# One step list for gates, heads and page products in a decoder kernel, with squares added in pairs and page numbers read in four parts

## The chip, the cores and the metric

The kernel runs on one core of one Trainium2 chip. The time is device microseconds of one execution; 1627.98 us is the median of three runs of the kernel before (1627.06 to 1630.11). One further execution was taken with the hardware profiler, and all rows below are from it.

## What is computed

Two layers of a decoder trunk, run in one step on 256 tokens of one prompt and 4 new tokens of each of 8 samples (288 columns in all), D = 1024. Everything is float32.

```python
x += 0.5 * SwiGLU_1(rmsnorm(x))                         # FF = 2816
h = rmsnorm(x) @ w_in                                   # a_u, a_v, q, k, v, c_q, and three gates of 1024
u, v_n = gelu(a_u), layer_norm(gelu(a_v))
y_a = u * chunk_spatial_gate(v_n, s_w, s_b)             # 4 groups of 128, chunks of 128
y_b = moba_attention(rope(q), rope(k), v, past pages)   # 8 heads of 64; samples: 1024 past keys in pages of 128
y_c = cross_attention(c_q, memory keys, memory values)  # 4 heads of 128, 256 memory rows
g_a, g_b, g_c = split(sigmoid(gates), 3)
merged = g_a * (y_a @ w_a) + g_b * (y_b @ w_b) + g_c * (y_c @ w_c)
x += merged @ w_o
x += 0.5 * SwiGLU_2(rmsnorm(x))
```

After two layers a last rmsnorm gives y; new keys, values, memory keys and values and the samples' v_n are outputs too. `page_table` says which physical page of the cache each logical page of a sample is.

## The kernel before

All activations lie feature-major: 128 partitions, chunks of 288 columns. A weight matrix is walked in **units**: half a tile of 256 output columns by up to 1024 rows, 448 units for two layers (`layer_units`, 224 a layer). SP loads each unit into one of NR = 6 buffers (`load`), waiting until the unit six before it is used. ACT copies it rounded to the high half (`hi`, into one of NH = 4 buffers, L810), DVE subtracts for the low half (`lo`, L1110), and TensorE (`half`, L413) runs three matmuls of 288 columns per 128x128 block: high by high, low activation by high, high by low. A whole half tile is 24 matmuls; a half of w_a_out, w_b_out or w_c_out is 12. Results go to two pairs of PSUM banks, `res` slot 0 and slot 1; `evac[s]` counts how often slot s was taken, and the first matmul of a tile waits for it. Four more banks `gb` serve everything else in an order that `bank_uses` lists.

Each engine's order is its program's order: five programs, held together by semaphores alone. A layer is: feed-forward 1 (units 0 to 67), memory keys and values (68 to 75), the twelve tiles of w_in that are not gates (76 to 99, with the key pages of the samples between them), `attention_a` (100 to 115), `attention_c` (116 to 139), w_b_out (140 to 147), w_o (148 to 155), feed-forward 2 (156 to 223).

**The mean of squares.** ACT squares two chunks of x at a time into `work` (L830, `square`), 1/D included. When all four pairs are there DVE sums the eight chunks into `sqs` with one tensor_reduce (L1137, `sum_squares`), at the head of the next stage; TensorE sums over partitions with one float32 matmul against ones (L447, `sum_of`) placed behind the first tile of that stage. The same form serves layer norm (L1345, L1364) and the memory (L1168).

**attention_a** has 14 steps. In step n TensorE computes the scores of head n (L669), then one third of a gate step (two half tiles of a gate of branch a in slot 0, then the w_a_out tile in slot 1, for g = 0 to 3), then transposes the probabilities of head n-1 (L476), a quad of memory pages, and the output of head n-2 (L689, L697). Steps 12 and 13 finish heads 10 and 11 and have no gate work. DVE per step: scale the scores and find their maximum (L1424 or L1426, L1428), invert the sum and normalise the head before (L1440, L1442), the low half of a weight unit or the gate times branch product (L1451), copy a head's output out (L1460). ACT per step: weights' high half or sigmoid of the gate (L821), exp (L1010), copy of the transposed probabilities (L1021). Sigmoid, exp and sqrt each want their table loaded first.

The branch input goes through `high` (ACT, L984) and `y_low` (DVE, L1394), and w_a_out's first tile waits for `y_lo`. **attention_c** does the same for the memory branch (12 thirds of gate steps), with one quad of value pages beside each, then the four gate tiles of branch b, then waits for `y_lo` of the attention branch. DVE `select(1)` chooses the blocks of the second group of samples between the two.

**w_b_out, w_o.** Each w_b_out tile goes DVE product, DVE sum into `merged` (L1548, L1551), ACT high half (L1070), DVE low half (`merged_low`, L1538), between `hi` and `lo` of coming units. The first half tile of w_o needs the first two groups of merged (`m_lo` 2), the second all four.

**Pages.** A quad is four pages of 256 KB for four samples; `HOMES` gives the buffer of each. SP loads 24 quads a layer between weight units (`quad`, at unit numbers written out in `A_AT` and `C_AT`), POOL 16. Page numbers are read into SP's registers once, all eight quads' worth of two groups in a row, behind the load of unit 12 of layer 0 (L1590).

Of the kernel before, what the change touches and what calls it, by code (L numbers as in the profile page):

```python
# [6 lines left out]
F32 = mybir.dt.float32  # L7
# [6 lines left out]
P = 128  # L14
# [74 lines left out]
FFN_UNITS, LAYER_UNITS = 68, 224  # L89
U_MEM, U_QK, U_SLOT, U_GA, U_GC, U_SIGB, U_BRB, U_WO, U_FFN2 = 68, 76, 84, 100, 116, 132, 140, 148, 156  # L90
DOWN_NK = [8, 8, 6]
SLOT_TILES = [8, 9, 2, 3, 0, 1, 10, 11]


def layer_units():
# [12 lines left out]
    def gate(j, g):  # L108
        return tile("w_in", g + (GATE0 + j * D) // W)
# [8 lines left out]
    for j, name in ((0, "w_a_out"), (2, "w_c_out")):  # L118
        for g in range(4):
            u += gate(j, g) + tile(name, g, 0, 4)  # L120
    for g in range(4):
        u += gate(1, g)
    for g in range(4):
        u += tile("w_b_out", g, 0, 4)
    for t in range(4):
        u += tile("w_o", t)
# [24 lines left out]
HOME_NAMES = ("X", "Y", "Q0", "Q1", "Q2", "Q3", "W")  # L151

# [20 lines left out]
def bank_uses():  # L173

    def layer(L):
# [6 lines left out]
        for n in range(HEADS + 2):  # L182
# [5 lines left out]
            u += [("mo1", 3)] if n == 10 else []  # L188
            u += [(f"O{n - 2}", 2)] if n >= 2 and (n >= 10 or n % 2 == 0) else []
        u += [("moT", 0), ("oG0", 2), ("pTa1", 0), ("pTb1", 1), ("pTn1", 3), ("oT0", 0), ("oG1", 2), ("oT1", 0), ("rs2", 1)]  # L190
# [30 lines left out]
def build(nc, A):  # L221
# [158 lines left out]
    def _(pe):  # L380
# [62 lines left out]
        def sum_of(name, n, count):  # L443

            claim(name)
            pe.wait_ge(*count)
            pe.matmul(bk(name)[:, 0:n], ones, sqs[:, 0:n], start=True, stop=True).then_inc(filled_of(name), 1)  # L447

        def ffn(L, f):
            F = 2 * L + f - 1  # L450
            for i in range(UP):
                tile(0, 8, normed, ready=(lambda k: pe.wait_ge(norm_ready, 8 * F + k + 1)) if i == 0 else None)
                if i == 0:
                    if F == 0:
                        pe.wait_ge(ld_const, 16)
                    sum_of(f"rs{f}.{L}", T, (sqs_ready, 3 * L + (1 if f == 1 else 3)))
                if i == 2 and F == 0:
                    claim("memsum.0")
                    pe.wait_ge(memsum_ready, 1)
                    pe.matmul(bk("memsum.0")[:, 0:MEM], ones, mrstd[:], start=True, stop=True)\  # L460
                        .then_inc(filled_of("memsum.0"), 1)
# [56 lines left out]
        def mix(L):  # L518
# [17 lines left out]
            sum_of(f"rsm.{L}", T, (sqs_ready, 3 * L + 2))  # L536
# [61 lines left out]
            sum_of(f"ln1.{L}", T, (ln_sum, 2 * L + 1))  # L598
# [6 lines left out]
            sum_of(f"ln2.{L}", T, (ln_sum, 2 * L + 2))  # L605
# [28 lines left out]
            attention_a(L, spatial)  # L634
            attention_c(L)
# [13 lines left out]
        def gate_step(L, m, j, nth):  # L649

            if m % 3 < 2:
# [1134 lines left out]
```

## Time and profile before

| | |
|---|---|
| median of 3 runs | 1627.98 us (1627.06 to 1630.11) |
| the profiled execution | 1631.34 us, span of its trace 1629.7 us |
| TensorE busy | 1554.3 us (95%) |
| DVE, ACT, POOL busy | 916.8, 697.2, 80.9 us |
| mean granted TensorE clock | 0.976 of full |
| chain that ended last, by engine | TensorE 89%, DVE 6%, ACT 2% |

The page gives busy time, a row of 40 slices, the chain of work that ended last, and the costliest groups of instructions with the idle time just before them and who ended it. Views of the trace give the same for a stretch, an engine or a tile, and the instructions one by one. Start times are microseconds from the start of the span. A matmul's busy time includes its way through the array, so the pace of matmuls is read from their starts.

### The profile page before, as it was taken

The page shows a single profiled execution, that of the slowest core. Times are in us where ns is not written, and L with a number is a line of the kernel's source. Part 1 is how long each engine was busy: PE and PEld are TensorE (multiplying, and loading weights), DVE is VectorE, ACT ScalarE, POOL GpSimd, SP SyncE. Part 2 cuts the span into 40 slices and gives each one's busy share as a digit, 9 for nine tenths or more (in the row PEclk, how much of TensorE's full clock was granted, in tenths as well). Part 3 has the DMA queues.
Part 4 walks back from the last instruction along what each step waited for, and adds up shares of the span by engine and source line. Part 5 has one row for each costly group of instructions (what it writes and reads, how often), then busy time and mean ns, then how long its engine had stood idle before and what let it go on. Part 6 is the DMA issues. An engine that isn't in the chain of part 4 may idle for free.

```text
span 1629.7 us, 28853 instructions
## 1 busy us (share of the span) xinstructions
PE 1554.3 (95%) x12164; PEld 1470.2 (90%) x12164; DVE 916.8 (56%) x1169; ACT 697.2 (43%) x907; POOL 80.9 (5%) x153
## 2 busy tenths in 40 slices
PE   7799999999999989999999999999999997999996
PEld 7799999997877889999999999999977777999996
DVE  6566447564644366665466654665656435755644
ACT  6344335354543344444344443433555333544432
POOL 0000000130003000000000000004000210000000
PEclk9899999999999999999999999999999998999998
DMA  6345658695479344445544456759655853444552
GB/s 246 117 165 160 208 178 288 237 329 167 155 251 337 107 159 153 165 168 155 168 166 161 166 188 191 240 196 350 232 181 175 324 207 130 155 161 164 161 166 78
DMA packets 106001, 313.86 MB, mean 193 GB/s; under 512 B 12880, under 2 KB 12880, under 8 KB 105744
## 3 DMA queue, kind: packets, MB, share of 16 engines
q1 hardware_dynamic: 94320, 273.87, 50.5%
q0 software_dynamic: 11552, 38.15, 6.3%
q8 instruction: 96, 1.57, 0.4%
q14 instruction: 33, 0.27, 0.1%
HBM read 306.20 MB, written 5.77 MB: 191 GB/s over the span
## 4 chain that ended last, share of the span: by engine, by line
PE 89%; DVE 6%; ACT 2%; issue 1%; SPq 1%; DMA 1%; DVEq 0%; ACTq 0%
PE res L413 76%; PE gb L497 2%; PE gb L506 2%; DVE square_sums L1137 2%; PE gb L669 2%; PE res L435 1%; PE gb L476 1%; ACT whi L810 1%; DVE wlo L1110 1%; DMA wraw<-in_ffn_w 1%; SPq L1590 1%; PE gb L697 1%; PE gb L689 1%; PE gb L489 1%; PE gb L447 1%
## 5 line engine op out<-in xcount | busy, mean ns | idle before, releaser
L1110 DVE TENSOR_TENSOR wlo<-wraw,whi 128x1024 fp32r<-128x1024 f32 (+2 forms) x448 | 512.0, 1148 | 552.9 <-ACT whi L810 551.9
L413 PE MATMUL res<-norm_hi,whi 128*128 128x288 f32 x2176 | 659.8, 303 | 21.0 <-DVE wlo L1110 10.0
L810 ACT ACTIVATE whi<-wraw 128x1024 fp32r<-128x1024 f32 (+2 forms) x448 | 443.5, 994 | 540.2 <-PE res L413 497.8
L413 PE MATMUL res<-norm_lo,whi 128*128 128x288 f32 x2176 | 646.3, 297 | 0.0
L413 PE MATMUL res<-norm_hi,wlo 128*128 128x288 f32 x2176 | 644.1, 296 | 0.0
L413 PEld LDWEIGHTS res<-norm_hi,whi 128*128 128x128 f32 x2176 | 412.6, 190 | 48.4 <-issue 24.0
L413 PEld LDWEIGHTS res<-norm_lo,whi 128*128 128x128 f32 x2176 | 413.3, 190 | 1.1
L413 PEld LDWEIGHTS res<-norm_hi,wlo 128*128 128x128 f32 x2176 | 413.9, 190 | 0.0
L413 PE MATMUL res<-h_hi,whi 128*128 128x288 f32 x1024 | 311.3, 304 | 22.3 <-DVE h_lo L1394 13.1
L413 PE MATMUL res<-h_lo,whi 128*128 128x288 f32 x1024 | 307.9, 301 | 0.0
L413 PE MATMUL res<-h_hi,wlo 128*128 128x288 f32 x1024 | 307.2, 300 | 0.0
L413 PEld LDWEIGHTS res<-h_hi,whi 128*128 128x128 f32 x1024 | 197.7, 193 | 31.9 <-DVE h_lo L1394 14.3
L413 PEld LDWEIGHTS res<-h_hi,wlo 128*128 128x128 f32 x1024 | 198.3, 194 | 0.0
L413 PEld LDWEIGHTS res<-h_lo,whi 128*128 128x128 f32 x1024 | 198.0, 193 | 0.1
L871 ACT ACTIVATE h_hi<-hf 128x576 fp32r<-128x576 f32 x44 | 30.2, 687 | 96.6 <-DVE hf L1188 96.6
L856 ACT ACTIVATE sil<-scaled 128x576 f32<-128x576 f32 x44 | 30.2, 685 | 86.5 <-DVE scaled L1165 86.5
L1010 ACT ACTIVATE soft<-soft,stat 128x256 f32<-128x256 f32 x48 | 24.1, 502 | 39.5 <-DVE stat L1428 39.4
L1679 POOL MEMSET q_blockdiag<- 128x512 f32 x8 | 3.9, 523 | 624.9 <-DVE h_lo L1150 619.1
L830 ACT ACTIVATE work<-x_T 128x576 f32<-128x576 f32 x28 | 18.7, 676 | 35.2 <-DVE x_T L1132 35.2
L1150 DVE TENSOR_TENSOR h_lo<-hf,h_hi 128x576 fp32r<-128x576 f32 x44 | 33.1, 752 | 0.0
L1165 DVE TENSOR_TENSOR scaled<-res,rstd 128x576 f32<-128x576 f32 x44 | 33.0, 750 | 0.1
L1132 DVE SCALAR_TENSOR_TENSOR x_T<-res,x_T 128x288 f32<-128x288 f32 x48 | 19.7, 452 | 23.7 <-PE res L413 23.5
(189 smaller groups left out, 1125.1 us busy)
## 6 DMA issues: line engine op xcount, KB each, us to landing
wraw<-in_ffn_w SPq DMA_DIRECT2D x240, 512.0 KB, 3.5
wraw<-in_w_in SPq DMA_DIRECT2D x96, 512.0 KB, 5.0
wraw<-in_ffn_w SPq DMA_DIRECT2D x32, 384.0 KB, 3.2
page_Q<-in_cache_k POOLq DMA_DIRECT2D x48, 256.0 KB, 5.1
page_Q<-in_cache_k SPq DMA_DIRECT2D x40, 256.0 KB, 5.0
page_Q<-in_cache_v SPq DMA_DIRECT2D x40, 256.0 KB, 5.4
wraw<-in_w_mem_kv SPq DMA_DIRECT2D x16, 512.0 KB, 3.4
page_Q<-in_cache_v POOLq DMA_DIRECT2D x32, 256.0 KB, 5.1
```

The costliest lines, as they stand in the source:

```text
L413: mm = pe.matmul(res[:, 2 * s + c, 0:n], w_, m_, start=begin and k == 0 and j == 0, stop=end and k == kh - 1 and j == 2)
L497: mm = pe.matmul(bk(name)[32 * e:32 * e + 32, col:col + P], q_[:, c, e, :], page[b][e][:, c * P:(c + 1) * P], start=c == 0, stop=c == 3)
L506: mm = pe.matmul(bk(name)[32 * e:32 * e + 32, :], probs[:, 32 * e:32 * e + 32], page[b][e][:], start=begin, stop=end)
L669: mm = pe.matmul(bk(nm)[:, qt * 256:(qt + 1) * 256], lhs, rhs, start=True, stop=True)
L810: act.activation(whi[n % NH][:, 0:kh, :], wraw[n % NR][:, 0:kh, :], ACT.Copy).then_inc(hi_done, 1)
L856: act.activation(sil[:], scaled[:], ACT.Silu).then_inc(sil_ready, 1)
L871: act.activation(hh[:, 2 * i:2 * i + 2, :], hf[:], ACT.Copy).then_inc(hh_ready, 1)
L1010: a = act.activation(soft[n % 2][:, qt, :], soft[n % 2][:, qt, :], ACT.Exp, bias=stat[:, 4 * (n % 2) + qt:4 * (n % 2) + qt + 1], accum_out ...
L1110: dve.tensor_tensor(wlo[n % NR][:, 0:kh, :], wraw[n % NR][:, 0:kh, :], whi[n % NH][:, 0:kh, :].bitcast(F32), ALU.subtract).then_inc(lo_don ...
L1137: dve.tensor_reduce(sqs[:], work[:, 0:chunks, :].rearrange("p k t -> p t k"), AX.X, ALU.add).then_inc(sqs_ready, 1)
L1150: dve.tensor_tensor(hl[:, 2 * i:2 * i + 2, :], hf[:], hh[:, 2 * i:2 * i + 2, :].bitcast(F32), ALU.subtract)\
L1165: dve.tensor_tensor(scaled[:], rs(0), both(rstd[:]), ALU.mult).then_inc(evac[0], 1)
```

## The change

**One step list.** `attention_a` and `attention_c` become one loop `gates` over 32 steps (`STEPS`): capital letters are half gate tiles, small letters whole branch tiles. Per branch two gates (four halves) come first, and each product stands behind a later gate. Heads are steps 0 to 11, their tails fall in steps 12 and 13 beside the gates of the memory branch; value quads are steps 12 to 19 and 21 to 28; the last memory product (c, 3) moves behind the gates of b. The weight units are laid out in this order. Branch b's input takes the place of branch a's in h. SP's places for quads come from the last use of each buffer (`load_after`). DVE takes a head's output one step later, `spatial` behind the normalising of a head, `y_low` for branch a in step 3, ACT's `high` for it in step 2.

**Squares in pairs.** `sum_squares` goes. DVE adds pairs of chunks into the first pair as they come (`add_squares`): group 1 behind the third tile of the projection, group 2 behind the fourth, group 3 at the head of the next stage. TensorE sums over partitions with two matmuls. Layer norm's two sums and the memory's go the same way. At the end the third group's sum is done as before by TensorE, and a Sqrt on one column is put ahead of the last `deviation`.

**Page numbers in four parts**, behind the loads of units 12, 16, 20 and 24 of layer 0; the loads of sgu_b and sgu_w move to unit 28.

**Also**: w_o's halves run (0,0) (1,0) (0,1) (1,1) and then as before, and the new x is taken at the halves where a tile ends; at the start each weight unit's halves follow one pair of chunks of x, not two; memory's high and low halves are made two per pass in passes 6 to 9 of feed-forward 1, not one in passes 3 to 10, and the memory is scaled in pass 3, not 2.

```diff
+def gate_steps(b):
+    two = [(b, g, h) for g in range(2) for h in range(2)]
+    return two + [(b.lower(), 0, None), (b, 2, 0), (b, 2, 1), (b.lower(), 1, None), (b, 3, 0), (b, 3, 1), (b.lower(), 2, None),
+                  (b.lower(), 3, None)]
+
+
+STEPS = gate_steps("A") + gate_steps("C")[:-1] + [("B", g, h) for g in range(4) for h in range(2)] + [("c", 3, None)]
+N_STEPS = len(STEPS)
+WO_ORDER = [(0, 0), (1, 0), (0, 1), (1, 1), (2, 0), (2, 1), (3, 0), (3, 1)]
...
+QUAD_STEP = {Q_MK + i: 1 + i for i in range(4)}
+QUAD_STEP.update({Q_MV + i: 8 + i for i in range(4)})
+QUAD_STEP.update({Q_V + i: 12 + i + i // 8 for i in range(16)})
+
+
+def quad_unit(q):
+    return U_SLOT + q if q < Q_MK else step_unit(QUAD_STEP[q] + 1) - 1
+
+
+FIRST_LOAD = {0: 46, 1: 52, 2: 74, 3: 75, 4: 76, 5: 77, 11: 96}
+
+
+def load_after(q):
+
+    if q in FIRST_LOAD:
+        return FIRST_LOAD[q]
+    prev = max(p for p in range(q) if HOMES[p] == HOMES[q])
+    free = quad_unit(prev)
+    if q == Q_V + 3:
+        free = step_unit(12) - 1
+    if q == Q_V + 4:
+        free = step_unit(14) - 1
+    return free + NR
...
-        def sum_of(name, n, count):
+        def sum_of(name, src, n, *ready):
 
             claim(name)
-            pe.wait_ge(*count)
-            pe.matmul(bk(name)[:, 0:n], ones, sqs[:, 0:n], start=True, stop=True).then_inc(filled_of(name), 1)
+            pe.wait_ge(*ready)
+            for k in range(2):
+                mm = pe.matmul(bk(name)[:, 0:n], ones, src[:, k, 0:n], start=k == 0, stop=k == 1)
+            mm.then_inc(filled_of(name), 1)
...
+            for n in range(N_STEPS):
+                kind, g, h = STEPS[n]
+                assert unit[0] == LAYER_UNITS * L + step_unit(n)
                 if n < HEADS:
                     head_scores(n)
-                    gate_step(L, n, 0, 1)
+                if kind in "AC":
+                    half(0, h, 8, normed)
+                elif kind == "B":
+                    half(g % 2, h, 8, normed)
+                else:
+                    pe.wait_ge(y_lo, 3 * L + (1 if kind == "a" else 2))
+                    tile(1, 4, branch(0 if kind == "a" else 1))
...
             pe.wait_ge(y_lo, 3 * L + 3)
             for g in range(4):
-                tile(g % 2, 4, branch(1))
-            for t in range(4):
-                for h in range(2):
-                    if t == 0:
-                        pe.wait_ge(m_lo, 4 * L + 2 * h + 2)
-                    half(t % 2, h, 8, lambda k: (hh[:, 8 + k, :], hl[:, 8 + k, :]))
+                tile(g % 2, 4, branch(0))
+            for t, h in WO_ORDER:
+                if t < 2:
+                    pe.wait_ge(m_lo, 4 * L + 2 * h + 2)
+                half(t % 2, h, 8, lambda k: (hh[:, 8 + k, :], hl[:, 8 + k, :]))
...
+        def gates(L):
+            branches = tiles[1]
+            for n in range(N_STEPS + 1):
+                if n:
+                    kind, g, h = STEPS[n - 1]
+                    u = LAYER_UNITS * L + step_unit(n - 1)
+                    if kind in "AC":
+                        if h == 0:
+                            hi(u + 4)
+                        else:
+                            k = g + (0 if kind == "A" else 4)
+                            if k >= 2:
+                                act.wait_ge(evac[1], branches + k - 1)
+                            if k == 1:
+                                act.wait_ge(out_vn, 16 * (L + 1))
+                            take(u, 0, gsil[k % 2][:], ACT.Sigmoid)
+                            hi(u + 4)
+                    elif kind == "B":
+                        if h == 1:
+                            take(u, g % 2, sig_b[g // 2][:, 2 * (g % 2):2 * (g % 2) + 2, :], ACT.Sigmoid)
                         hi(u + 4)
...
-        def sum_squares(stage, chunks=KD):
-
-            dve.wait_ge(sq_ready, 4 * stage + chunks // 2)
-            dve.tensor_reduce(sqs[:], work[:, 0:chunks, :].rearrange("p k t -> p t k"), AX.X, ALU.add).then_inc(sqs_ready, 1)
+        def add_squares(stage, g, last=3):
+
+            dve.wait_ge(sq_ready, 4 * stage + g + 1)
+            i = dve.tensor_tensor(work[:, 0:2, :], work[:, 0:2, :], work[:, 2 * g:2 * g + 2, :], ALU.add)
+            if g == last:
+                i.then_inc(sqs_ready, 1)
+            else:
+                step(i)
...
+            def product(g, kind):
+
+                k = g + (0 if kind == "a" else 4)
+                dve.wait_ge(evac[0], gates_before + k + 1)
+                to = acc[:, 2 * g:2 * g + 2, :]
+                tiles[1] += 1
+                if kind == "a":
+                    dve.tensor_tensor(to, gsil[k % 2][:], rs(1), ALU.mult).then_inc(evac[1], 1)
+                else:
+                    dve.tensor_tensor(scaled[:], gsil[k % 2][:], rs(1), ALU.mult).then_inc(evac[1], 1)
+                    dve.wait_ge(evac[1], tiles[1])
+                    step(dve.tensor_tensor(to, to, scaled[:], ALU.add))
...
+                if n in (10, 12):
+                    mem_rows((n - 10) // 2)
                 if 1 <= n <= HEADS:
...
+                if n:
+                    kind, g, h = STEPS[n - 1]
+                    u = LAYER_UNITS * L + step_unit(n - 1)
+                    if kind in "AC":
+                        lo(u + 4)
+                        tiles[0] += h
+                    elif kind == "B":
+                        lo(u + 4)
+                        tiles[g % 2] += h
                     else:
...
+                        done(u + 1)
+                        product(g, kind)
+                        lo(u + 4)
+                        lo(u + 5)
...
-                if n == b + 12:
-                    if L == 0:
-                        for i in range(0, HELD, 2):
-                            held += ids_of(i, 2)
+                if L == 0 and n in (12, 16, 20, 24):
+                    held += ids_of(n // 2 - 6, 2)
+                if n == b + 28:
```

## Rows read from the trace of the kernel before

**Rows 1.** The page: busy us, share of the span and instructions by engine

```profile
PE 1554.3 (95%) x12164; PEld 1470.2 (90%) x12164; DVE 916.8 (56%) x1169; ACT 697.2 (43%) x907; POOL 80.9 (5%) x153
```

**Rows 2.** Stretches: length; busy us (instructions) of PE, PEld, DVE, ACT, POOL; clock; DMA; GB/s

```profile
80.00:230.00 150.00, 150.00 (x1128) 150.00 (x1127) 85.21 (x94) 63.53 (x75) 0.99 (x2) 1.00 0.56 179
```

**Rows 3.** The same view, stretches in which TensorE loses time

```profile
54.00:78.00 24.00, 12.98 (x71) 12.68 (x71) 12.43 (x11) 9.25 (x10) 0.00 (x0) 0.72 0.53 176
247.00:250.50 3.50, 1.08 (x8) 0.80 (x7) 3.50 (x2) 2.83 (x3) 0.00 (x0) 1.00 0.97 290
...
826.00:832.00 6.00, 3.67 (x15) 3.24 (x14) 6.00 (x4) 4.13 (x4) 0.00 (x0) 0.72 0.25 90
...
1181.50:1194.00 12.50, 9.03 (x67) 8.05 (x66) 6.22 (x10) 6.87 (x10) 0.00 (x0) 0.73 0.45 147
456.00:467.00 11.00, 8.49 (x33) 6.94 (x34) 7.34 (x20) 1.19 (x3) 0.00 (x0) 0.69 0.75 242
...
554.00:562.50 8.50, 4.74 (x24) 4.50 (x23) 2.74 (x3) 2.85 (x4) 0.00 (x0) 0.80 0.17 49
...
572.00:586.50 14.50, 9.89 (x55) 9.45 (x54) 9.19 (x11) 4.21 (x6) 0.00 (x0) 0.76 0.43 145
```

**Rows 4.** Waits of TensorE: who waited for whom, total us, times, longest

```profile
PE res L413 <- DVE h_lo L1394: 13.1, 4, 3.8
...
PE res L413 <- DVE h_lo L1538: 8.3, 2, 4.2
```

**Rows 5.** The chain that ended last, 30 to 80: start, us, what

```profile
38.05 1.94 SPq L1590
...
54.62 5.54 DMA wraw<-in_ffn_w
```

**Rows 6.** DVE groups by line: count, busy us, mean ns, idle before

```profile
L1137 DVE TENSOR_REDUCE square_sums<-work 128x288 f32<-128x2304 f32 (+1 forms) x7 | 28.4, 4061 | 1.1 <-ACT work L830 1.1
```

**Rows 7.** Instructions in order of time, DVE at head 9: start, us, what

```profile
438.32 0.69 DVE L1426 TENSOR_SCALAR soft<-gb 128x512 f32<-128x512 f32 x1 [3.04 <-PE gb L669]
...
440.37 0.75 DVE L1451 TENSOR_TENSOR merged<-gate_sigmoid,res 128x576 f32<-128x576 f32 x1
```

**Rows 8.** The same view, TensorE at a sum and at two float32 matmuls

```profile
249.81 0.72 PE L447 MATMUL gb<-square_sums,consts 128*128 128x288 f32 x2 [2.42 <-DVE square_sums L1137]
...
250.49 0.28 PE L413 MATMUL res<-mem_lo,whi 128*128 128x256 f32 x1
...
299.26 1.24 PE L489 MATMUL gb<-work,consts 128*128 128x288 f32 x4
...
300.46 0.29 PE L413 MATMUL res<-norm_lo,whi 128*128 128x288 f32 x1
```

**Rows 9.** The same view, DVE at the end

```profile
1615.88 3.07 DVE L1137 TENSOR_REDUCE square_sums<-work 128x288 f32<-128x1728 f32 x1
```

**Rows 10.** The same view, the start

```profile
6.78 0.96 ACT L834 ACTIVATE norm_hi<-x_T,gains 128x288 fp32r<-128x288 f32 x2 [1.58 <-DMA x_T<-in_x_T]
...
20.95 0.72 PE L447 MATMUL gb<-square_sums,consts 128*128 128x288 f32 x2 [1.59 <-DVE square_sums L1137]
```

**Rows 11.** The same view, TensorE and DVE at w_b_out and w_o of layer 0

```profile
558.13 0.40 PE L413 MATMUL res<-h_hi,whi 128*128 128x288 f32 x1 [3.76 <-DVE h_lo L1394]
...
572.30 0.74 DVE L1548 TENSOR_TENSOR scaled<-gate_b,res 128x576 f32<-128x576 f32 x1
...
577.35 0.74 DVE L1548 TENSOR_TENSOR scaled<-gate_b,res 128x576 f32<-128x576 f32 x1
...
579.94 0.75 DVE L1538 TENSOR_TENSOR h_lo<-merged,h_hi 128x576 fp32r<-128x576 f32 x1
```

**Rows 12.** The same view, ACT at a gate

```profile
430.71 1.28 ACT L821 ACT_TABLE_LOAD   x1
432.01 0.65 ACT L821 ACTIVATE gate_sigmoid<-res 128x576 f32<-128x576 f32 x1
```

**Rows 13.** The page: DMA issues, count, KB each, median us from issue to landing

```profile
page_Q<-in_cache_v SPq DMA_DIRECT2D x40, 256.0 KB, 5.4
```

## Working and prediction

> **What bounds it now.** I read the page first: TensorE is busy 1554.3 of 1629.7 us [rows 1], so the matmuls set the time and only TensorE's idle time, its slow stretches and its work can change it. Next came stage windows. In the first feed-forward of layer 0 (and just so in the others) 1128 matmuls run in 150.00 us without idle at the full clock [rows 2]: 0.133 us each, 3.19 us for a half tile of 24. Nothing is to be had there. Then I looked for stretches with less than that, and priced each as its length less its matmuls at 0.133 us. That counts idle time and the stretch at the lower clock level (1.2 of 2.4 GHz) that follows some of it. The rows [rows 3] are to be read so: 54 to 78 us holds 71 matmuls, so 24.0 - 9.4 = 14.6 us are lost; 826 to 832 holds 15, 4.0 lost; 247 to 250.5 holds 8, 2.4 lost at a full clock. The waits say whose fault it is: DVE's low halves of the branch inputs (L1394) and of the merged sum (L1538) [rows 4].
>
> **The change part by part.**
>
> *Page numbers in four parts.* The chain shows SP reading the numbers from 38.05 us on and the next weight load only at 54.62, landing 5.54 us later [rows 5]. Nothing is loaded in between, TensorE runs dry, 14.6 us go. One part is a quarter of the 16.6, some 4.1 us. A load may be issued six units (19 us) before its own turn; 4.1 late, 5.54 to land and some 2.5 for its two conversions make 12. Four units lie between parts. I take 14.6 as gained; the ends are 0 (loads never catch up) and 14.6. The two bias loads move behind them, to unit 28, needed much later.
>
> *Squares added in pairs.* Before, DVE reduces eight chunks in one instruction, 4.06 us on the mean over seven [rows 6], after the last square; TensorE stands for it 2.4 us (247) or, with the slow stretch, 4.0 us (826) [rows 3]. There are five such places: three lose 2.3 to 2.4, two 4.0; 15.0 in all. After, two of three additions are done earlier, between tiles where DVE has idle time, and the last, one 128x576 sum, costs 0.75 us [rows 7]: it is done before the first tile of the next stage is, so nothing waits. What is late next is the matmul itself: there are now two chunks to sum over. One such sum holds TensorE 0.56 us (249.81 to 0.12 before 250.49), two back to back 1.07 (299.26 to 0.13 before 300.46) [rows 8]: 0.51 more for each of 10 sums and some 0.5 for the memory's, +5.6. DVE's own saving elsewhere (layer norm, memory) hides behind TensorE and is worth nothing; nor do the memory's halves cost anything that now come two to a pass in four passes instead of one in eight, with its scaling a pass later: DVE is busy 85 and ACT 64 of 150 us there [rows 2]. At the very end the reduce of 3.07 us [rows 9] becomes 0.75, less 0.51 for one matmul more: 1.8 gained. The table load put ahead there had been hidden already: nothing.
>
> *The start.* ACT waited 1.58 us for the second chunk of x before it made the first weights' high half [rows 10]; now that half goes first. Bounds 0 and 1.58 plus the 1.59 that TensorE waited for the first sum [rows 10]; I take 2.7, since each piece of that order is then bound by loads only a little earlier.
>
> *The step list.* Four places per layer lose time, priced from layer 0 (layer 1 repeats each within 0.1 us). (a) The first branch product waits for y's low half, and one head's transposes just before it wait too: 1181.5 to 1194 (the row of layer 1, which holds both) has 3.5 idle and 0.27 x 12.5 = 3.4 of clock; a little of the slow stretch lies in the idle one, so 6.7. It now stands behind four gate halves, and y's low half is made a step earlier than its product needs it, by some 2 us. (b) Heads 10 and 11 had no gate halves beside them: 456 to 467, 2.5 idle, 3.4 of clock, of which I take 5.8. They now have the memory gates beside them. (c) 554 to 562.5, waiting for the last y: 8.5 - 24 x 0.133 = 5.3. The last memory product (3.19 us) now lies between. (d) 572 to 586.5: 14.5 - 55 x 0.133 = 7.2 [rows 3]. Twice 25.0 is 50.0.
>
> For (d) I don't take the whole. First tile of w_b_out at 558.13; DVE lets go of the first bank at 573.04 (572.30 + 0.74), of the second at 578.09, and has the last low half at 580.69 [rows 11]: 14.9, 20.0 and 22.6 after the start. This ladder of DVE and ACT (two low halves of weights, product, sum, low half, with ACT's high half between) is not touched. It comes some 1.4 earlier as the first tile no longer runs at the lower clock: 13.5, 18.6, 21.2. TensorE has four tiles, 12.8, waits 0.7 for the bank, 3.2, waits for the second bank from 16.7 to 18.6, ends at 21.8, and no longer waits for the last low half. So 2.6 idle stays; the clock costs between 0 (as at 247) and 3.4 (as at 1181) with it, I take 1.0. New loss 3.6 a layer, 7.2.
>
> The list also makes new waits, which I looked for where two tiles in a row use one bank pair. *The products a2 and a3 stand next to each other, both in bank pair 1.* a3 can't start until DVE has taken a2, and DVE's step first scales the scores of head 11, which TensorE computes just ahead of a3, finds their maximum and normalises head 10. The same run of DVE at head 9 goes from 438.32 to the end of the product at 441.12 [rows 7]: 2.8, with the signal 2.9 us of TensorE idle. Behind a3 in its queue stand head 10's transposes; ACT waits for those to copy them, DVE only a step later, so all three come 2.9 late together. The clock then costs 1.7 (as at 554) or 3.4 (as at 1181); I take 2.5. 5.4 a layer, 10.8. *The second gate follows the first in bank pair 0* while ACT must load its sigmoid table (1.28) and take the tile (0.65) [rows 12] behind the copy of head 0's probabilities: some 0.45 is not covered. *The last B gate and c3 share bank pair 1*: the bare 0.65 and two signals, 0.8. With odds and ends of 0.3, 1.55 a layer, 3.1.
>
> A rule of the Trainium skill bears on the second gate. In the rows the sigmoid starts 1.30 us after its table load does [rows 12]. The Trainium skill, page "ScalarE: Activation LUTs", section "What ACT_TABLE_LOAD costs", gives a switch 2.66 us, a drain of 1.38 behind the load included. By that the wait would be 1.8 instead of 0.45 and the whole 2.8 us longer; the row speaks against it.
>
> The quads that SP and POOL load are placed by new units, each behind the use before it in its buffer; the nearest has three steps of about 4.4 us to land 5.4 [rows 13]. SP's own wait before the one quad that lies over the softmax buffers (head 11 must be out) was there before; behind it stand weight loads with six units to spare. I cost them at nothing; if that cover is gone, each of 32 value quads can hold TensorE for up to 1.0 (5.4 - 4.4).
>
> **The sum.** Gained: 14.6 + 15.0 + 1.8 + 2.7 + 50.0 = 84.1. Given back: 5.6 + 7.2 + 10.8 + 3.1 = 26.7. Net 57 us. The profiled execution took 1631.3 us (span 1629.7 and 1.6 around it), 0.2% over the median of the three runs, 1627.98; I take the 57 off the median: 1571.
>
> **Rivals.**
> 1. *No new wait.* DVE gets to a2 before TensorE has head 11's scores, or the clock holds: only the 5.6 of matmuls are given back, 78 net, 1550. For it: 2.4 idle at 247 left the clock alone. Against: the order of DVE's step is written out, scores before product.
> 2. *The gates become bound by pages or by the DVE and ACT ladder.* All value quads land late, 32 x 1.0, and the clock falls in some: 30 to 40 lost, about 1605. For it: the same bytes in less time. Against: in the old profile no wait for a page shows among TensorE's.
> 3. *The page numbers still starve the loads*, or stand in front of a tile that counts: 14.6 not gained, 1586.
> 4. *Slower.* Every gate tile (12 a layer) shows ACT's table load and copy, 1.28 + 0.65 + 0.2 = 2.1 idle, and the clock falls each time (1.7 to 3.4): 24 x 4.7 = 113 lost, 1684. From 2.4 us a tile on it is slower than before. Against: table loads of the old order were as many and no wait for them shows among TensorE's.
>
> **How the numbers follow.** The forecast as summed, 1560 to 1582: 0.55. Rival 1: 0.14. Rival 2: 0.17. Rival 3: 0.09. Rival 4: 0.04. None at all, within 0.2% (about 3 us, what a measurement of this kernel can tell): 0.01. Faster 0.95, same 0.01, slower 0.04. The unknown clock costs (0 to 3.4 at each of four new places) make about 9 us either way; the range reaches to rival 1's 1550 and rivals 2 and 3 below 1598.
>
> **What would show it.** In the profile after: no TensorE idle between 40 and 80 us; each stage's sum between two tiles with no wait; no reduce at the stage ends. In each layer one idle stretch of about 2.9 us on a DVE product in the middle of the heads, the largest new one; two short ones at w_o's first and second half. Wrong if a step without a2 or a3 shows TensorE waiting for ACT's take, for a page, or for low halves of weights, or if TensorE's idle time apart from start and end is under 5 us or over 25.

## The result and the profile after

The changed kernel takes 1574.21 us (median of four runs, 1573.44 to 1575.62), the kernel before 1628.35 beside it (1627.06 to 1630.11): a ratio of 0.9668, 95% interval 0.9651 to 0.9685. That is 54.1 us less on the medians and 56.9 between the two profiled spans (1629.7 and 1572.8); I had forecast 57 and 1571. Direction and size were right. Some of the reasons weren't, and the runs below sort them. Between the two profiles TensorE's waits of 0.3 us or more fell from 66.8 to 27.1 us, and its time lost at the lower clock (counted as said below) from some 29 to 5 us; so some 24 us of the gain are clock that came back with the waits.

The page of the kernel after, TensorE's line: 17.6 us less busy than before [rows 1], and 98% of a shorter span.

```profile
PE 1536.7 (98%) x12188; PEld 1453.5 (92%) x12188; DVE 893.4 (57%) x1183; ACT 703.3 (45%) x912; POOL 80.9 (5%) x153
```

All waits of TensorE after (who, for whom: total us, times, longest), the successors of [rows 4]:

```profile
PE res L455 <- issue: 8.7, 6, 2.9
PE res L455 <- DVE wlo L1128: 8.6, 1, 8.6
PE res L455 <- DVE h_lo L1558: 3.2, 2, 1.6
PE res L455 <- DVE norm_lo L1254: 2.3, 2, 2.0
PE gb L818 <- DVE work L1155: 1.7, 1, 1.7
PE gb L490 <- DVE work L1155: 1.6, 1, 1.6
PE res L455 <- ACT gate_sigmoid L853: 0.9, 2, 0.5
```

The two big groups of before are gone (L1394's 13.1 us; L1538's 8.3, which is now L1558 with 3.2). "issue" is where the profile names nobody; by their places the six are the fourth product of branch a (2.9, twice), c3 (0.8, twice) and w_o's first half (0.6, twice). The one line the forecast had no place for is norm_lo, L1254.

Stretches after (length; busy us and instructions of PE, PEld, DVE, ACT, POOL; granted clock; DMA; GB/s), as in [rows 3]:

```profile
54.00:78.00 24.00, 24.00 (x182) 24.00 (x181) 17.98 (x18) 11.02 (x12) 0.00 (x0) 1.00 0.53 177
428.00:436.00 8.00, 5.07 (x26) 4.71 (x25) 5.33 (x9) 1.10 (x4) 0.00 (x0) 0.79 0.53 184
545.50:553.00 7.50, 5.24 (x38) 4.83 (x38) 6.86 (x9) 3.36 (x5) 0.00 (x0) 1.00 0.73 254
1022.00:1029.50 7.50, 5.55 (x31) 5.34 (x30) 5.46 (x6) 4.05 (x6) 0.73 (x1) 0.77 0.58 229
1205.00:1209.00 4.00, 1.06 (x8) 0.92 (x8) 3.71 (x7) 1.10 (x4) 0.00 (x0) 1.00 0.84 279
```

54 to 78 us holds 182 matmuls where 71 were: the hole is gone. Below, "lower clock" with a number is the time lost at it: one less the granted clock of half-microsecond stretches, times their length, summed over the stretches in which TensorE works. At 428 (fourth product, layer 0) it costs 1.7 us behind 2.93 idle; at 1205 (the same product, layer 1) the same idle time costs none; at w_o (545.5) none.

The fourth product, instruction by instruction (start, us, what, and the idle time before it):

```profile
428.42 0.69 DVE L1487 TENSOR_SCALAR soft<-gb 128x512 f32<-128x512 f32 x1 [2.82 <-PE gb L701]
...
430.47 0.75 DVE L1446 TENSOR_TENSOR merged<-gate_sigmoid,res 128x576 f32<-128x576 f32 x1
...
431.32 0.37 PE L455 MATMUL res<-h_hi,whi 128*128 128x288 f32 x1 [2.94 <-issue]
```

This is the chain that the forecast took from head 9 [rows 7]: DVE idles 2.8 us, scales head 11's scores, and only then takes the third product, for whose banks the fourth waits.

The start of layer 1's mixing stage, where the unforeseen wait is (SP's queue, then ACT, DVE and TensorE):

```profile
1011.69 1.90 SPq L1632 DMA_DIRECT2D page_Q<-in_cache_k  x4
1014.00 8.87 SPq L1606 DMA_DIRECT2D wraw<-in_w_in  x4
...
1020.75 1.06 ACT L842 ACTIVATE whi<-wraw 128x1024 fp32r<-128x1024 f32 x1 [5.37 <-DMA wraw<-in_w_in]
...
1022.20 1.24 ACT L926 ACTIVATE norm_hi<-work 128x576 fp32r<-128x576 f32 x2
...
1022.99 1.42 DVE L1254 TENSOR_TENSOR norm_lo<-work,norm_hi 128x576 fp32r<-128x576 f32 x2
...
1024.46 0.40 PE L455 MATMUL res<-norm_hi,whi 128*128 128x288 f32 x1 [1.95 <-DVE norm_lo L1254]
```

SP issues the last of four key quads ahead of the weights of w_in. ACT stands 5.37 us at a weight half that hasn't landed, and behind it in ACT's queue stand the high halves of the normalised x, which have nothing to do with that weight. In the kernel before, ACT stood at the same weight half too, but only for 1.80 us, and no wait of TensorE followed:

```profile
1057.40 1.06 ACT L810 ACTIVATE whi<-wraw 128x1024 fp32r<-128x1024 f32 x1 [1.80 <-DMA wraw<-in_w_in]
```

### The profile page after: what moved, and what is told of

Its sections match the earlier page's. It is cut to its first block, busy times and chain, and to the rows that moved or that the text cites. A ratio compares the mean times of both kernels' runs of the same rounds, so it can differ in the third digit from the quotient of the medians.

```text
span 1572.8 us, 28936 instructions
## 1 busy us (share of the span) xinstructions
PE 1536.7 (98%) x12188; PEld 1453.5 (92%) x12188; DVE 893.4 (57%) x1183; ACT 703.3 (45%) x912; POOL 80.9 (5%) x153
## 4 chain that ended last, share of the span: by engine, by line
PE 95%; DMA 2%; DVE 1%; issue 1%; ACT 1%; SPq 0%; DVEq 0%; ACTq 0%
PE res L455 83%; PE gb L547 3%; PE gb L538 2%; PE gb L701 1%; PE gb L517 1%; DMA wraw<-in_w_in 1%; PE gb L490 1%; PE gb L729 1%; PE gb L721 1%; PE gb L530 1%; ACT whi L842 0%; DMA wraw<-in_ffn_w 0%; PE gb L554 0%; PE gb L666 0%; PE gb L741 0%
## 5 line engine op out<-in xcount | busy, mean ns | idle before, releaser
L455 PE MATMUL res<-h_hi,whi 128*128 128x288 f32 x1024 | 305.6, 298 | 12.0 <-issue 8.7
L455 PE MATMUL res<-h_lo,whi 128*128 128x288 f32 x1024 | 302.7, 296 | 0.0
L455 PE MATMUL res<-h_hi,wlo 128*128 128x288 f32 x1024 | 302.0, 295 | 0.0
L455 PEld LDWEIGHTS res<-h_hi,whi 128*128 128x128 f32 x1024 | 192.6, 188 | 20.8 <-issue 15.0
L455 PEld LDWEIGHTS res<-h_hi,wlo 128*128 128x128 f32 x1024 | 193.4, 189 | 0.0
L455 PEld LDWEIGHTS res<-h_lo,whi 128*128 128x128 f32 x1024 | 193.0, 188 | 0.1
L1208 DVE TENSOR_TENSOR scaled<-sil,rstd 128x576 f32<-128x576 f32 x44 | 33.1, 752 | 0.0
```

Source lines behind the costliest of these rows:

```text
L455: mm = pe.matmul(res[:, 2 * s + c, 0:n], w_, m_, start=begin and k == 0 and j == 0, stop=end and k == kh - 1 and j == 2)
L1208: step(dve.tensor_tensor(scaled[:], sil[:], both(rstd[:]), ALU.mult))
```

## The experiments

All but no_step_list, which starts from the kernel before, start from the changed kernel (1574.21). ids_bias_mem, squares_start and five_fixes take several moves together, the others one. The runs were taken at different times, with the kernel before beside each; its median moved from 1628.4 to 1630.8. The differences below are between medians as they stand, so some 2.5 us of each can be that drift.

| run | median us (range) | ratio to before, 95% interval |
|---|---|---|
| ids_at_once | 1580.86 (1577.8 to 1584.22) | 0.970 (0.9685 to 0.9715) |
| ids_bias_mem | 1588.38 (1584.71 to 1591.9) | 0.9745 (0.9723 to 0.9766) |
| squares_in_one | 1594.60 (1594.23 to 1596.72) | 0.979 (0.9775 to 0.9805) |
| squares_start | 1593.07 (1590.39 to 1595.98) | 0.9777 (0.9761 to 0.9792) |
| start_old | 1573.97 (1570.64 to 1575.63) | 0.9646 (0.9632 to 0.9659) |
| no_step_list | 1603.16 (1598.51 to 1606.34) | 0.985 (0.9835 to 0.9865) |
| wo_old | 1582.23 (1582.14 to 1582.74) | 0.9702 (0.9689 to 0.9715) |
| product_first | 1566.16 (1563.78 to 1566.63) | 0.9613 (0.96 to 0.9626) |
| norms_first | 1570.28 (1569.67 to 1573.02) | 0.9636 (0.9622 to 0.965) |
| wo_ladder | 1568.21 (1566.26 to 1569.64) | 0.9617 (0.9604 to 0.9631) |
| one_chunk | 1570.75 (1569.7 to 1575.19) | 0.9645 (0.9628 to 0.9662) |
| five_fixes | 1554.48 (1551.43 to 1556.56) | 0.953 (0.9517 to 0.9544) |

### The page numbers

```diff
-                if L == 0 and n in (12, 16, 20, 24):
-                    held += ids_of(n // 2 - 6, 2)
+                if L == 0 and n == 12:
+                    for i in range(0, HELD, 2):
+                        held += ids_of(i, 2)
```

> The changed kernel (1574.2 us) with one part undone: all page numbers are read in one go behind unit 12 again; the two bias loads stay at unit 28. Theory: the 16.6 us in which SP reads starve the weight loads, TensorE loses 14.6 us between 50 and 80 us of the span, time 1588.8. Rival: it was the two bias loads queued behind the numbers that made the loads late; then less than half comes back, under 1581.

6.7 us more, not the 14.6 of the theory; under 1581, as the rival had it. But the median lies between two pairs of runs: 1577.8 and 1578.3 at a mean granted clock of 0.996, 1583.4 and 1584.2 at 0.992, so 3.6 to 10.0 us more. The trace is of the longest run. It has one wait, and 122 matmuls in the old hole: 24.0 - 122 x 0.133 = 7.8 us lost there. The wait begins at 52.6, before the stretch; whole, it and the lower clock behind it (3.0) make 9.4.

```profile
PE res L455 <- DVE scaled L1187: 6.4, 1, 6.4
```

```profile
54.00:78.00 24.00, 18.96 (x122) 18.96 (x123) 15.62 (x15) 12.06 (x13) 0.00 (x0) 0.79 0.55 187
```

The rest had to lie in what the change moves beside the numbers: the bias loads (`n == b + 28`) and the memory's scaling (DVE, pass 3). I undid these as well:

```diff
-                if n == b + 28:
+                if n == b + 12:
...
-                if F == 0 and i == 3:
+                if F == 0 and i == 2:
                     inverse_deviation("memsum.0")
```

> The changed kernel with the page numbers in one go, the two bias loads behind them at unit 12, and the memory scaled in pass 2, all as before. With the numbers alone undone, the trace showed one wait of 6.4 us and 3 of clock. Theory: the 14.6 us that I put down to the numbers had two more parts: the bias loads and a slower landing put the wait up to 9.2, and DVE's inverse and scaling of the memory (1.75 and 2.29 us) in the pass after it made a second wait of 1.9 with a stretch at the lower clock; then both waits are back and 54 to 78 us holds about 71 to 80 matmuls where the numbers alone left 122. Rival: the numbers alone are all there is, and the stretch looks as with them alone.

14.2 us more, and the old picture: 79 matmuls (13.5 lost in the stretch; 15.1 with the whole first wait, which begins at 52.5) and two waits.

```profile
54.00:78.00 24.00, 13.92 (x79) 13.69 (x80) 13.33 (x12) 9.53 (x11) 0.00 (x0) 0.72 0.50 169
```

```profile
PE res L455 <- DVE scaled L1187: 9.5, 1, 9.5
...
PE res L455 <- DVE hf L1212: 2.1, 1, 2.1
```

The second wait is DVE's: just when TensorE has its weights again, DVE inverts and scales the memory, 4.0 us of work ahead of the low half and of hf, for which TensorE waits.

```profile
64.48 1.75 DVE L1165 RECIPROCAL mem_rstd<-mem_rstd 128x256 f32<-128x256 f32 x1 [2.54 <-ACT mem_rstd L859]
66.27 2.29 DVE L1194 TENSOR_TENSOR memn_T<-memn_T,mem_rstd 128x2048 f32<-128x2048 f32 x1
```

So the 14.6 were one hole with more than one cause; the numbers alone make 3.6 to 10.0 us of it, by the run, and 9.4 of 15.1 between the two traces. The bias loads and the scaling weren't tried apart. By the traces the first weight behind the numbers is issued 0.8 us later with the bias loads ahead of it, and lands in 6.3 us instead of 4.1, which together make the longer first wait (9.5 for 6.4); that the bias loads slow the landing is argued, not shown. The second wait (2.1, and 1.7 of lower clock) goes with the scaling. The weight in ids_at_once, then in ids_bias_mem:

```profile
51.88 4.11 DMA wraw<-in_ffn_w
```

```profile
52.64 6.30 DMA wraw<-in_ffn_w
```

### The sums of squares and the start

```diff
-            dve.wait_ge(sq_ready, 4 * stage + g + 1)
-            i = dve.tensor_tensor(work[:, 0:2, :], work[:, 0:2, :], work[:, 2 * g:2 * g + 2, :], ALU.add)
+            if g < last:
+                return
+            dve.wait_ge(sq_ready, 4 * stage + g + 1)
+            dve.tensor_reduce(sqs[:], work[:, 0:2 * g + 2, :].rearrange("p k t -> p t k"), AX.X, ALU.add).then_inc(sqs_ready, 1)
```

> The changed kernel with the sums of squares of the stages and of the end undone: one DVE reduce over eight chunks (six at the end) at the head of the stage, one matmul over partitions. Layer norm's and the memory's sums stay in pairs. By the forecast's terms 15.0 + 1.8 come back and six matmuls of 0.51 (3.1) go: 13.7 more, 1587.9. Second theory, from the trace after: at the two memory stages the wait for norm_lo (0.38 and 1.95 idle with 1.71 of clock, 4.0) stands where the sum's wait was, so those 4.0 were not gained and go again: 9.7 more, 1583.9. Rival: DVE's reduce is hidden now, under 3 more, 1577.

20.4 us more; both theories were too small, and the rival further off. The waits for the sum are back at all six stage heads and at the end:

```profile
PE gb L490 <- DVE square_sums L1159: 15.8, 6, 4.0
...
PE gb L820 <- DVE square_sums L1159: 4.0, 1, 4.0
```

The longest, 4.0, is a place where the kernel before lost 1.6 [rows 10]: the very first sum. It now starts at 21.32, with 3.3 us of lower clock behind it.

```profile
21.32 1.30 PE L490 MATMUL gb<-square_sums,consts 128*128 128x288 f32 x2 [3.98 <-DVE square_sums L1159]
```

Between the two profiles (22.2 us apart) TensorE's waits grow by 13.7 us and the lower clock by 11.4, and the single matmuls give some 3 back. Of the 11.4, 3.3 stand behind the first sum, 5.1 behind three of the other heads and 1.3 at the end; the rest falls in places that this kernel doesn't change. The first theory had 3.4 of clock in all. The new order of the first weights doesn't make up for the missing pairs. Then what does that order bring?

```diff
-            hi(g)
+            if g % 2:
+                hi(g - 1)
+                hi(g)
```

(and the same for `lo` on DVE)

> The changed kernel with the first weights' halves made in the old order, after every second pair of chunks of x. The forecast gave this order 2.7 us. With the sums in one reduce and the new order the first sum began at 21.32 us, in the kernel before at 20.95, in the changed kernel at 18.27. Theory: the 2.7 come from the pairs, not from the order; here the sum begins at 18.3 to 18.8 and the time is within 1 of 1574.2. Rival: the order brings its 2.7: 1576.9.

1573.97, no difference that these runs can tell; the rival's 2.7 more is out. The first sum starts at 19.16, 0.9 later than in the changed kernel and a little later than the theory said, but TensorE doesn't wait for it at all; it only begins its first tile later (11.3 for 8.6).

```profile
19.16 1.13 PE L490 MATMUL gb<-work,consts 128*128 128x288 f32 x4
```

Both together:

> The changed kernel with both the sums in one reduce (as in the run that undid them alone, 1594.6) and the old order of the halves at the start. Theory: of the 20.4 us that undoing the sums cost, 3.8 stood at the start alone, where the new order without the pairs put the first sum at 21.32 us with 3.4 us of lower clock behind it; here the sum begins at about 20.95 as in the kernel before, with no lower clock, and the time is 1590.8. Rival: the start has no part in the 20.4, same time as with the sums undone alone, 1594.6.

1593.07: the start behaves as the theory has it (the sum at 20.60, no lower clock there), but the median falls by 1.5 us only, less than the runs' range. The start's part in the 20.4 is thus not shown by the times. Against start_old the sums are worth 19.1 on the medians and 15.8 between the profiled spans (1588.7 and 1572.9); the difference goes with how often the clock falls, which varies from run to run.

### The step list

The kernel before with all parts but `gates`, `STEPS` and `WO_ORDER`.

> The kernel before (1628.35) with every part of the change but the step list and the new order of w_o's halves: squares in pairs, page numbers in four parts, the start, the memory's halves, the last table load. Distance to the changed kernel is what the list is worth. By the forecast 50.0 less 21.1 = 28.9: 1603.1. By the waits that the trace after shows in the list's stages (2 x 2.93 and 1.71 of clock at the third and fourth product, 4.5 at w_o, 0.95 and 1.57 at the gates: 14.6) it is 35.4: 1609.6. Rival: most of the gain came from the other parts, under 1594.

1603.16, so the list with w_o's order is worth 28.95 us, against 28.9 forecast. The four runs spread over 8 us (24 to 32 for the list), so an agreement this close is luck. The second theory's 1609.6 lies 3.3 above the longest of them, and the rival's 1594 below the shortest. The waits are those of [rows 4], each to the tenth, and the heads':

```profile
PE res L413 <- DVE h_lo L1401: 13.1, 4, 3.8
PE res L413 <- DVE h_lo L1545: 8.3, 2, 4.2
...
PE gb L475 <- DVE soft L1449: 5.2, 4, 1.9
```

The order of w_o's halves alone, undone:

```diff
-WO_ORDER = [(0, 0), (1, 0), (0, 1), (1, 1), (2, 0), (2, 1), (3, 0), (3, 1)]
+WO_ORDER = [(t, h) for t in range(4) for h in range(2)]
```

> The changed kernel with w_o's halves in the old order (both halves of a tile one after the other), so that the second half needs all of merged's low halves. From the trace after: the first half tile starts at 546.65, ends at 549.85, DVE's last low half ends at 554.2; the wait is 4.4 where 1.63 was: 2.8 more in each layer, and if the clock falls behind it another 1.7 to 3.4. Theory: 5.6 to 12.4 more, 1579.8 to 1586.6. Rival: the ladder's end sets w_o whatever the order, same time, 1574.

8.0 us more, within the theory's 5.6 to 12.4: 2 x 2.5 of idle time, and the lower clock is back in both layers (1.7 and 2.6). The wait at the second half:

```profile
554.87 0.61 PE L455 MATMUL res<-h_hi,whi 128*128 128x288 f32 x1 [4.17 <-DVE h_lo L1558]
```

### The waits that the change made or uncovered

```diff
             for n in range(N_STEPS + 1):
+                if n == 11:
+                    done(LAYER_UNITS * L + step_unit(10) + 1)
+                    product(2, "a")
```

(and not at its old place in that step)

> The changed kernel with one move: in the step of head 11 DVE takes the third product of branch a before it scales that head's scores, not after. Theory: the fourth product no longer waits, 2 x 2.93 idle and 1.71 of clock go, 7.6 less, 1566.6, and no TensorE wait appears instead. Rival: the softmax of heads 10 and 11 is the limit of this place; then the same 2.9 us show at the next transposes and the time stays at 1574.

8.0 us less. DVE takes the product in the 2.8 us in which it stood idle; the waits without a name fall from 8.7 to 2.8 us, and no lower clock remains in the two layers of this profile. (At norm_lo that isn't the move's doing: the wait there is 2.6 us, longer than in the changed kernel, and the clock held.) A wait of 0.3 us for DVE's copy of a head's output is new in each layer, where the theory had none.

```profile
426.19 0.74 DVE L1446 TENSOR_TENSOR merged<-gate_sigmoid,res 128x576 f32<-128x576 f32 x1
429.09 0.69 DVE L1490 TENSOR_SCALAR soft<-gb 128x512 f32<-128x512 f32 x1 [2.16 <-PE gb L701]
```

```profile
PE res L455 <- issue: 2.8, 4, 0.8
```

The memory stage:

```diff
-            mem_tile(2, mvrow[:, :, 0:W])
+            hi(m + 8)
             normal(2)
             normal(3)
+            hi(m + 9)
+            take(m + 5, 0, mvrow[:, :, 0:W], ACT.Copy, MEM)
```

(and `normal_low(2)`, `normal_low(3)` ahead of `lo(m + 9)` on DVE)

> The changed kernel with one move in the memory stage: ACT's high halves and DVE's low halves of the third and fourth group of the normalised x come ahead of the weight half that waits for a late load, not behind it. Theory: the trace after has TensorE wait 0.38 and 1.95 us for norm_lo, with 1.71 of clock in layer 1, because ACT stands 3.5 and 5.4 us at a weight that four key quads in SP's queue have delayed; with the move the waits go, 4.0 less, 1570.2. Rival: TensorE then waits for that late weight itself, and the time stays at 1574.

3.9 us less, and no wait for norm_lo. ACT still stands at the late weight, but with nothing urgent behind it. How much the move saves depends on the run: in six other profiles that leave this stage alone the waits for norm_lo are 0.7 to 2.8 us in all, and in none of them does lower clock follow.

```profile
1014.54 1.26 ACT L926 ACTIVATE norm_hi<-work 128x576 fp32r<-128x576 f32 x2
1019.76 1.06 ACT L842 ACTIVATE whi<-wraw 128x1024 fp32r<-128x1024 f32 x1 [3.96 <-DMA wraw<-in_w_in]
```

w_o's ladder:

```diff
-                lo(u0 + 2 * g + 4)
+                if g < 2:
+                    lo(u0 + 2 * g + 4)
                 if g:
                     merged_low(g - 1)
...
+                if g == 2:
+                    lo(u0 + 8)
                 taken(s)
...
+                if g == 3:
+                    lo(u0 + 10)
+                    merged_low(3)
```

> The changed kernel with DVE's order at the third and fourth w_b_out tile changed: low half of merged and the gate product first, the low halves of the weights for w_o after them. Theory: the 0.63 and 1.63 us that TensorE waits at w_o's first and second half in each layer are DVE's order alone; both go, 4.5 less, 1569.7. Rival: the low halves of w_o's weights, now later, are waited for instead: no gain, 1574, or some us more.

6.0 us less, 4.5 of it the waits that were forecast to go; where the rest lies isn't shown. h_lo has left the waits; DVE has the last product at 548.02 where it was at 550.86.

```profile
547.36 0.75 DVE L1558 TENSOR_TENSOR h_lo<-merged,h_hi 128x576 fp32r<-128x576 f32 x1
548.02 0.75 DVE L1569 TENSOR_TENSOR scaled<-gate_b,res 128x576 f32<-128x576 f32 x1
```

The price of a float32 matmul:

```diff
-            for k in range(2):
-                mm = pe.matmul(bk(name)[:, 0:n], ones, src[:, k, 0:n], start=k == 0, stop=k == 1)
+            pe.matmul(bk(name)[:, 0:n], ones, src[:, 0, 0:n], start=True, stop=True).then_inc(filled_of(name), 1)
...
+                step(i)
+                i = dve.tensor_tensor(work[:, 0, :], work[:, 0, :], work[:, 1, :], ALU.add)
```

> The changed kernel with one more DVE addition of 128x288 for each sum of squares, so that TensorE sums over partitions with one matmul, not two (11 sums; the last one of all is left). Theory: each float32 matmul holds TensorE for 0.51 us, by the forecast: 5.6 less, 1568.6; the addition of some 0.4 us is hidden everywhere but at the first sum, +0.4. Rival: the added step on DVE is on the path at the stage heads, 11 x 0.4 come back, and the time stays at 1574.

This kernel sums only one of two chunks for layer norm's mean: DVE's addition is left out there, and TensorE's work is the same as with it. 3.5 us less, between the two. TensorE's busy time falls by 4.2 us. The addition costs DVE 0.46, and the waits for norm_lo are 3.1 us in all for 2.3; as they differ by as much between kernels that change nothing there, that the addition makes them longer isn't shown:

```profile
230.96 0.46 DVE L1156 TENSOR_TENSOR work<-work 128x288 f32<-128x288 f32 x1
```

```profile
PE res L455 <- DVE norm_lo L1256: 3.1, 2, 2.2
```

Everything together (one_chunk's addition whole, and at the very end the third pair of squares added before the last tile is taken):

> The changed kernel with the three moves measured one by one (the product first: 8.0 less; the norms first: 3.9 less; DVE's order at w_o: 6.0 less), one matmul per sum of squares (3.5 less when alone, here with layer norm's first sum whole), and one more: at the very end DVE adds the third pair of squares before the last tile is taken, so that TensorE's two matmuls over it stand before the last wait, some 1.0 less. Theory: the five places are apart from each other and add up: 22.4 less, 1551.8. Rival: with these waits gone others come up behind them (pages, late weights, the clock), and half is given back, 1563.

1554.48: 19.7 us less than the changed kernel, of 22.4 expected (22.2, if each is taken from the kernel before beside it), and 4.7% under the kernel before. So the five places add up, and the rival's 1563 is out. What TensorE still waits for is the start and less than 5 us elsewhere:

```profile
PE res L455 <- DVE wlo L1128: 8.3, 1, 8.3
PE gb L489 <- DVE work L1158: 2.5, 1, 2.5
PE res L455 <- issue: 1.6, 2, 0.8
PE res L455 <- ACT gate_sigmoid L851: 0.9, 2, 0.5
PE gb L819 <- ACT work L860: 0.7, 1, 0.7
PE gb L727 <- DVE cq_T L1537: 0.6, 2, 0.3
```

## Why the prediction held, step by step

*Page numbers.* The term, 14.6, was right (14.2 when undone, 10.5 to 17.7 by the run); the step that gave all of it to the 16.6 us of reading was not: the reading alone cost 3.6 to 10.0 (ids_at_once), and the 16.6 held the issue of the bias loads too, from 53.77 to 54.62. I costed the memory's scaling "a pass later" and the moved bias loads at nothing, because their neighbourhood at the full pace has idle time on DVE [rows 2]. But the hole isn't at that pace: there the scaling, free elsewhere, stood ahead of what TensorE waited for.

*Sums.* The five waits went. "So nothing waits; what is late next is the matmul itself" failed at the memory stage of both layers: 2.4 and 2.4 plus 1.7 of lower clock before were replaced by 0.38 and by 1.95 plus 1.71 on norm_lo. I had looked at the chain that feeds the sum, not at what the old wait had been giving time to: four quads in SP's queue and a weight behind them. In layer 1 SP issued the four over 13.2 us before and over 9.5 after, and the weight landed late. norms_first prices it at 3.9 us, about the 3.2 by which the forecast was too low. Against that the sums as a whole were worth more than the 13.7 put on what squares_in_one undid: 15.8 to 20.4. Most of the surplus is lower clock behind the waits that came back, which I had priced from one profile (3.4) and which is 9.6 at the sums in squares_in_one's; what it costs behind a wait differs from run to run.

*Matmuls of float32.* Two now hold TensorE for some 0.97 to 1.07 us, 0.41 to 0.51 more than one; forecast 0.51. Taking one away gave 3.5 of the 5.6.

*Start.* 2.7 was the right distance for the first sum (20.95 to 18.27), by luck, as the reason was wrong: undoing the order changes the time by 0.2 us, and without the pairs the order makes the first sum later than before.

*Step list.* Its worth was forecast at 28.9 and measured at 28.95. The new waits were found where the forecast put them: the fourth product 2.93 (2.9), w_o 0.63 and 1.63 (0.7 and 1.9), c3 0.79 (0.8), the second gate 0.47 (0.45). The mis-sized term is the clock at w_o, 1.0 taken twice: no profile with that wait shows any. At the fourth product I took 2.5 twice. The profile after shows 1.7 and 0, and 1.7 more in a stretch 13.7 us behind the first wait; over ten profiles it is 1.4 a place, and 2.3 with such later stretches, if they belong to it. The wait at w_o was also not a fixed ladder, as I had it: DVE's order alone was worth 6.0.

*The parts together.* Undone one by one, the page numbers with their neighbours, the sums, the start and the list are worth 14.2, 20.4, -0.2 and 28.95 us: 63.3, where the whole change gave 54.1 and the second matmuls of layer norm and memory, some 2.5 by the forecast, would take back a part. So the parts don't add, and that the total came within 3.2 us of the forecast doesn't show that each term is right. What makes up the difference is open; the spread of the runs and the lower clock are in it. The memory's halves and the early table load weren't tried alone. At the end, from the last tile to the end of the span, 14.56 us became 12.43: 2.1 gained for 1.8 forecast.

*The gate and the table load.* In layer 0 the second gate's table load starts at 369.85, its sigmoid at 371.14, 1.29 us later, and TensorE waits 0.47.

```profile
369.85 1.28 ACT L853 ACT_TABLE_LOAD   x1
371.14 0.65 ACT L853 ACTIVATE gate_sigmoid<-res 128x576 f32<-128x576 f32 x1
```

The Trainium skill, page "ScalarE: Activation LUTs", section "What ACT_TABLE_LOAD costs", gives 2.66 us for a switch, by which, as an estimate, that wait would have been 1.8. This trace doesn't agree: its load and the step to the sigmoid take 1.29 us in all.

*Rivals.* No wait for a page shows on TensorE (rival 2), none for the numbers (rival 3), and the other gate tiles show no exposed take (rival 4). Rival 1 was out: the fourth product waited as written. Apart from the start and the end TensorE's waits are some 15 us (17 with the first sum's), within the 5 to 25 I had set.

## What to carry to other kernels

When a wait is removed, look at every queue that it had been giving time to, not only at the chain that fed it: ACT stood 5.37 us at a late weight where it had stood 1.80. In an engine's written order, put what another engine is waiting for ahead of whatever may block, even for the length of a scale and a maximum; three such moves here gave 8.0, 6.0 and 3.9 us for no work saved. A hole in the trace can have several causes in a row, and undoing one part shows the share of that one only; shares found one by one needn't add up to the whole.

## What was not expected of the hardware

The same idle time costs the clock differently. Over ten profiles with the fourth product's wait, 2.93 or 2.94 us in both layers, the stretch after it ran at 1.2 GHz for a loss of about 1.7 us in 15 of 20 places, 3.3 in one, and stayed at 2.4 GHz in four. The 1.62 or 1.63 us waits at w_o were never followed by a slow stretch in nine profiles. A stretch can also be slow with no idle time ahead of it: after, 445 to 449 us, TensorE is busy all 4.00 us with page products and transposes, at a granted clock of 0.57.

```profile
445.00:449.00 4.00, 4.00 (x16) 2.01 (x16) 0.12 (x1) 0.00 (x0) 0.00 (x0) 0.57 0.80 275
```

Such a stretch, 1.7 us of loss each, stands 12 to 14 us behind the wait in 10 of the 20 places, in two of them where the clock had held behind the wait itself. In the two profiles without the wait (product_first and five_fixes) it isn't there; that the wait causes it isn't shown. Times of single runs differ by a few us with such stretches; what makes the difference stays open.
